# Expert gate and up products as three single-pass products of high and low parts, with one set of weight buffers and a new order of the jobs

## The reference, cut to what matters

```python
def hier_moe(h, w_rg, w_re, w_gate, w_up, w_down):      # h: tokens x 1024
    g_idx = jnp.argmax(h @ w_rg, axis=-1)               # best of 4 groups
    ...
    top_v, top_i = lax.top_k(e_in_group, TOP_K)         # best 2 of its 8 experts
    w = jax.nn.softmax(top_v, axis=-1) * g_w
    flat_e = (g_idx[:, None] * EXPERTS_PER_GROUP + top_i).reshape(-1)
    order = jnp.argsort(flat_e)
    ...
    a = lax.ragged_dot(xs, w_gate, sizes)               # 1024 -> 512 of each row's own expert, 32 experts
    u = lax.ragged_dot(xs, w_up, sizes)                 # 1024 -> 512
    y = lax.ragged_dot(jax.nn.silu(a) * u, w_down, sizes)   # 512 -> 1024
    y = y * w.reshape(-1)[order][:, None].astype(y.dtype)
    return jax.ops.segment_sum(y, tok, num_segments=n)
```

## Time and profile before

| What | us |
|---|---|
| Median of three runs | 6089.7 |
| The profiled execution, its own time | 6090.85 |
| Its span in the trace | 6089.3 |
| TensorE busy | 5199.9 |
| VectorE busy | 2233.9 |
| ScalarE busy | 1677.5 |
| GpSimd busy | 821.7 |

### The profile page before, as it was taken

One profiled execution on the slowest core, in us unless ns is written; L12 is line 12 of the kernel. 1 busy time (PEld: TensorE's weight loads), 2 busy tenths in 40 slices (PEclk: granted clock), 3 DMA queues, 4 the chain that ended last, 5 costly groups with the idle time before them and its releaser, 6 DMA issues. The chain is left out here.

```text
span 6089.3 us, 76302 instructions
## 1 busy us (share of the span) xinstructions
PE 5199.9 (85%) x27165; PEld 3869.3 (64%) x27165; DVE 2233.9 (37%) x4438; ACT 1677.5 (28%) x2876; POOL 821.7 (13%) x1023
## 2 busy tenths in 40 slices
PE   9588899779789885999991888979879886999995
PEld 1388889669668763444441888978778665444442
DVE  0455155566443432111115552547553333111113
ACT  0244254446322320000001342536542221000000
POOL 0244200440000001000001440006200001000001
PEclk9799999899899997999995999989889998999998
DMA  8432451324332464899976432233343343999997
GB/s 320 175 92 88 145 172 47 95 72 111 135 147 98 167 202 165 326 335 334 334 281 229 144 95 78 68 81 78 90 134 114 143 148 110 343 334 335 334 334 265
DMA packets 610733, 1111.26 MB, mean 182 GB/s; under 512 B 108400, under 2 KB 291984, under 8 KB 610032
## 3 DMA queue, kind: packets, MB, share of 16 engines
q1 hardware_dynamic: 565104, 956.50, 47.0%
q0 software_dynamic: 29504, 94.50, 4.0%
q10 hardware_dynamic: 15936, 57.78, 2.3%
HBM read 908.23 MB, written 200.45 MB: 182 GB/s over the span
## 5 line engine op out<-in xcount | busy, mean ns | idle before, releaser
L642 PE MATMUL project_proj_acc<-project_w_split,project_hT 128*128 128x256 f32 x5472 | 720.0, 291 | 41.0 <-DVE project_w_split L527 41.0
L642 PEld LDWEIGHTS project_proj_acc<-project_w_split,project_hT 128*128 128x128 f32 x5472 | 689.5, 198 | 42.1 <-DVE project_w_split L527 41.8
L1452 PE MATMUL merge_acc<-merge_hT,merge_w_split 128*128 128x512 f32 (+1 forms) x2880 | 633.4, 376 | 20.0 <-issue 16.8
L1452 PEld LDWEIGHTS merge_acc<-merge_hT,merge_w_split 128*128 128x128 f32 x2880 | 507.9, 190 | 128.9 <-issue 22.0
L2059 PE MATMUL experts_gate_acc<-experts_w_gate,experts_rowsT 128*128 128x512 f32 x1184 | 526.0, 597 | 6.9 <-DMA experts_w_up<-in_w_exp_up_dram 6.9
L2046 PE MATMUL experts_result_acc<-experts_w_down,experts_hiddenT 128*128 128x512 f32 x1184 | 520.5, 592 | 2.4 <-DVE experts_hiddenT L2018 2.4
L2064 PE MATMUL experts_up_acc<-experts_w_up,experts_rowsT 128*128 128x512 f32 x1184 | 520.2, 592 | 0.0
L2064 PEld LDWEIGHTS experts_up_acc<-experts_w_up,experts_rowsT 128*128 128x128 f32 x1184 | 225.0, 190 | 283.2 <-issue 283.2
L2010 DVE TENSOR_TENSOR experts_hidden<-experts_silu_gate,experts_up_acc 128x512 f32<-128x512 f32 x74 | 50.9, 688 | 964.5 <-PE experts_up_acc L2064 515.4
L2059 PEld LDWEIGHTS experts_gate_acc<-experts_w_gate,experts_rowsT 128*128 128x128 f32 x1184 | 221.2, 192 | 259.1 <-issue 257.4
L2046 PEld LDWEIGHTS experts_result_acc<-experts_w_down,experts_hiddenT 128*128 128x128 f32 x1184 | 219.3, 190 | 251.6 <-issue 248.7
(11 more groups left out here) (207 smaller groups left out, 7401.2 us busy)
## 6 DMA issues: line engine op xcount, KB each, us to landing
experts_w_gate<-in_w_exp_gate_dram SPq DMA_DIRECT2D x74, 2048.0 KB, 13.8
experts_w_up<-in_w_exp_up_dram SPq DMA_DIRECT2D x74, 2048.0 KB, 18.8
experts_w_down<-in_w_exp_down_dram SPq DMA_DIRECT2D x74, 2048.0 KB, 9.8
merge_w_raw<-in_w_merge_dram SPq DMA_DIRECT2D x120, 768.0 KB, 6.6
modulation_w_ada<-in_w_ada_dram SPq DMA_DIRECT2D x24, 2048.0 KB, 7.8
qk<-project_staged SPq DMA_DIRECT2D x168, 256.0 KB, 2.3
ye<-experts_result ACTq DMA_DIRECT2D x74, 512.0 KB, 8.2
ye<-attend_a_zeros POOLq DMA_DIRECT2D x52, 512.0 KB, 27.3
```

The lines of the kernel that those rows point to most:

```text
L642: m = pe.matmul(acc[s % 4][:, 0:HALF], hT[:, a, k, t * P:(t + 1) * P], w_split[hf][:, c, k, :], start=(i == 0 and k == 0), stop=(i == 2 an ...
L1452: m = pe.matmul(acc[:, bank, 0:w], w_split[b][:, a, k0 + k, :], act_T[:, x, kk, 0:w], start=(i == 0 and k == 0), stop=(i == 2 and k == n - 1))
```

## The change

The two sets of weight buffers go. There is now one buffer per weight, `raw`, in two halves of 1 MB, each with its own load and semaphore, and beside it one fp32r buffer `w` for gate and one for up that holds high and low parts. ScalarE casts each half to the high part, VectorE subtracts to get the low part, and TensorE makes 24 single-pass matmuls for gate and 24 for up; down stays in fp32 and reads `raw` itself. The transposed rows get high and low parts too. ScalarE alone now copies the result.

The raw buffers outlive `deal_rows`, which loads the three weights of expert 0 for job 0. For this the first 32 jobs are fixed as the first 128 rows of experts 0 to 31, and only the further tiles of larger experts are listed behind them; `deal_rows` gets some more VectorE steps for it. GpSimd issues the gathers of jobs 0 and 1 ahead of its loop.

```diff
 SP in deal_rows
+            for n in range(3):
+                for half in range(2):
+                    sp.dma_start(raw[n][:, half, :], expert_half(io, l, slice(0, 1), n, half)
+                                 ).then_inc(raw_in[n][half].sem, 16)
 VectorE in deal_rows
-            step(dve.tensor_scalar(base[:, :], base[:, :], float(P), None, ALU.mult))
-            step(dve.tensor_tensor(place[:, :, :], acc[:, 0:nq, :],
+            step(dve.tensor_tensor(base[:, :], base[:, :], small[:, C_JOB:C_JOB + NE], ALU.subtract))
+            step(dve.tensor_scalar(base[:, :], base[:, :], float(NE - 1), float(P), ALU.add, ALU.mult))
+            step(dve.tensor_scalar(place[:, :, :], acc[:, 0:nq, :], float(P), None, ALU.is_ge))
+            step(dve.tensor_tensor(place[:, :, :], place[:, :, :],
+                                   base[:, :].unsqueeze(1).to_broadcast([P, nq, NE]), ALU.mult))
+            step(dve.tensor_tensor(place[:, :, :], acc[:, 0:nq, :], place[:, :, :], ALU.add))
+            step(dve.tensor_scalar(base[:, :], small[:, C_JOB:C_JOB + NE], float(P), None, ALU.mult))
+            step(dve.tensor_tensor(place[:, :, :], place[:, :, :],
 run_experts
-    lo, hi = nq, MAX_JOBS // 2
-    w_gate = [sb(f"w_gate{b}", [P, KD, EH]) for b in range(2)]
-    w_up = [sb(f"w_up{b}", [P, KD, EH]) for b in range(2)]
-    w_down = [sb(f"w_down{b}", [P, HK, D]) for b in range(2)]
+    PASSES = ((0, 0), (1, 0), (0, 1))
+    lo, hi = NE // 2, MAX_JOBS // 2
+    w = [sb(f"w_{n}", [P, 2, 2, 2048], F32R) for n in ("gate", "up")]
 SP
-                    if later(g, 2):
-                        sp.wait_ge(um.sem, um.done(g - 2))
-                    for w, name in ((w_gate, "w_exp_gate"), (w_up, "w_exp_up")):
-                        sp.dma_start(w[b][:, :, :], io[name][l, ds(e, 1), :, :].rearrange(
-                            "o (k p) n -> p (o k) n", p=P)).then_inc(gu_in[b].sem, 16)
-                    if later(g, 2):
-                        sp.wait_ge(dm.sem, dm.done(g - 2))
+                    for n in range(3):
+                        for half in range(2):
+                            if n == DOWN:
+                                sp.wait_ge(dm.sem, dm.done(g - 1))
+                            else:
+                                sp.wait_ge(w_lo[n].sem, w_lo[n].done(g * 2 + half - 2))
+                            sp.dma_start(raw[n][:, half, :], expert_half(io, l, ds(e, 1), n, half)
+                                         ).then_inc(raw_in[n][half].sem, 16)
 ScalarE
+            def split(n, g):
+                if later(g, 1):
+                    act.wait_ge(products[n].sem, products[n].done(g - 1))
+                for half in range(2):
+                    act.wait_ge(raw_in[n][half].sem, raw_in[n][half].done(g))
+                    act.copy(w[n][:, 0, half, :], raw[n][:, half, :]).then_inc(w_hi[n].sem, 1)
...
                     act.activation(act_g[:, :], acc_g[:, :], ACT.Silu).then_inc(sg.sem, 1)
                     if not (last and b):
-                        copy_rows(g + 1)
+                        split(GATE, g + 1)
+                        rows_hi(g + 1)
+                        split(UP, g + 1)
 VectorE
+                    if not (last and b):
+                        split(GATE, g + 1)
                     dve.wait_ge(sg.sem, sg.done(g))
                     dve.wait_ge(um.sem, um.done(g))
...
                     dve.tensor_tensor(hidden[:, :], act_g[:, :], acc_u[:, :], ALU.mult).then_inc(hm.sem, 1)
                     if not (last and b):
-                        copy_rows(g + 1)
-                    if not isinstance(g, int) or g > 0:
-                        result(g - 1, 1 - b, i if b else i - 1)
+                        rows_lo(g + 1)
+                        split(UP, g + 1)
 TensorE
+            def into_hidden(n, acc, g):
+                for half in range(2):
+                    pe.wait_ge(w_lo[n].sem, w_lo[n].done(g * 2 + half))
+                    for i, (a, c) in enumerate(PASSES):
+                        for k in range(KD // 2):
+                            m = pe.matmul(acc[:, :], xT[:, a, half * (KD // 2) + k, :],
+                                          w[n][:, c, half, k * EH:(k + 1) * EH], start=(half == 0 and i == 0 and k == 0),
+                                          stop=(half == 1 and i == 2 and k == KD // 2 - 1))
+                m.then_inc(products[n].sem, 1)
...
-                    for k in range(KD):
-                        m = pe.matmul(acc_g[:, :], xT[:, k, :], w_gate[b][:, k, :], start=(k == 0), stop=(k == KD - 1))
-                    m.then_inc(gm.sem, 1)
+                    into_hidden(GATE, acc_g, g)
```

More of the change, by code:

```diff
@@ L1492, in stage_experts @@
             output_and_route(nc, io, scr, l, nq, st, inner, ident, logits)
[L1493 to L1496, removed]
+        with ExitStack() as weights:
+            raw = [st.sb(f"raw_{n}", [P, 2, 2048], F32, weights) for n in ("gate", "up", "down")]
+            raw_in = [[st.dma(f"raw_{n}{half}_loaded") for half in range(2)] for n in ("gate", "up", "down")]
+            with ExitStack() as inner:
+                deal_rows(nc, io, scr, l, nq, st, inner, logits, row_of, weight, jobs, more_pairs, raw, raw_in)
+            with ExitStack() as inner:
+                run_experts(nc, io, scr, l, nq, st, inner, ident, jobs, more_pairs, raw, raw_in)
         with ExitStack() as inner:
@@ L1816, in _ @@
             step(dve.tensor_copy(base[:, :], acc[:, nq, :]))
-            step(dve.tensor_tensor(more[:, :, :], base[:, :].unsqueeze(2).to_broadcast([P, NE, NT]),
-                                   small[:, C_TILE:C_TILE + NT].unsqueeze(1).to_broadcast([P, NE, NT]), ALU.is_gt))
+            step(dve.tensor_tensor(more[:, :, :], base[:, :].unsqueeze(2).to_broadcast([P, NE, NT - 1]),
+                                   small[:, C_TILE + 1:C_TILE + NT].unsqueeze(1).to_broadcast([P, NE, NT - 1]),
+                                   ALU.is_gt))
             step(dve.tensor_reduce(tiles[:, :], more[:, :, :], AX.X, ALU.add))
@@ L1870, in _, with expert_half, run_experts @@
             pool.wait_ge(scat.sem, scat.done(2 * nq - 1))
-def run_experts(nc, io, scr, l, nq, st, inner, ident, jobs, more_pairs):
+def expert_half(io, l, e, n, half):
+    w = io[("w_exp_gate", "w_exp_up", "w_exp_down")[n]]
+    rows = w.shape[2] // 2
+    return w[l, e, half * rows:(half + 1) * rows, :].rearrange("o (k p) n -> p (o k) n", p=P)
+def run_experts(nc, io, scr, l, nq, st, inner, ident, jobs, more_pairs, raw, raw_in):
     def sb(name, shape, dt=F32):
@@ L2035, in transpose_rows, with down @@
                 m.then_inc(xt.sem, 1)
-            def down(g, b, i):
+            def into_hidden(n, acc, g):
+                for half in range(2):
+                    pe.wait_ge(w_lo[n].sem, w_lo[n].done(g * 2 + half))
[5 more added lines that the diff above has]
+                m.then_inc(products[n].sem, 1)
+            def down(g):
                 pe.wait_ge(hc.sem, hc.done(g))
-                pe.wait_ge(d_in[b].sem, d_in[b].done(i))
-                if later(g, 1):
-                    pe.wait_ge(ya.sem, ya.done(g - 1))
                 if later(g, 1):
                     pe.wait_ge(yd.sem, yd.done(g - 1))
-                for h in range(D // 512):
-                    for k in range(HK):
-                        m = pe.matmul(acc_y[:, h * 512:(h + 1) * 512], hT[b][:, k, :],
-                                      w_down[b][:, k, h * 512:(h + 1) * 512], start=(k == 0), stop=(k == HK - 1))
+                for half in range(2):
+                    pe.wait_ge(raw_in[DOWN][half].sem, raw_in[DOWN][half].done(g))
+                    for c0 in range(D // 512):
+                        for k in range(HK // 2):
+                            m = pe.matmul(acc_y[:, c0 * 512:(c0 + 1) * 512], hT[:, half * (HK // 2) + k, :],
+                                          raw[DOWN][:, half, k * D + c0 * 512:k * D + (c0 + 1) * 512],
+                                          start=(half == 0 and k == 0), stop=(half == 1 and k == HK // 2 - 1))
                 m.then_inc(dm.sem, 1)
@@ L2076, in _ @@
             transpose_rows(0, 0, 0)
-            pairs(pe, n, body)
-            down(n * 2 - 1, 1, n - 1)
+            pairs(pe, n_pairs, body)
+            down(n_pairs * 2 - 1)
 def combine(nc, io, scr, l, nq, st, inner, row_of, weight, out):
```

144 lines of the change are left out of this document (75 added, 69 removed).

## The result

The changed kernel takes 7408.9 us, median of four runs (7400.3 to 7417.4); the kernel before, run beside it, takes 6089.0 (6085.6 to 6094.5, four runs). The ratio is 1.217, 95% interval 1.215 to 1.219. The forecast was 7450, range 7280 to 7620. The profiled execution took 7408.05 us, of which 7406.5 are span.

What follows compares the result with a forecast made beforehand. TensorE bounds the kernel before; the change puts load, split and TensorE's work in series. 2887.5 + 100 - 1630.8 + 4 = +1361, with 6090.85 giving 7452, less 1.2 for the median: 7450 us, range 7280 to 7620.

Steps and rivals of the forecast that it cites:

- SP's wait as the cause: SP's in-order queue: next gate and up loads stand behind the wait for down(g-1), putting load, split and products in series.
- The load, 0.15 + 13.4: After down(g-1) ends: SP wakes in 0.15 us, four halves (4 MB) land in 13.4, bounds 13.0 to 15.3.
- the rival in which all halves land together: Weight loads: engines shared among six halves, gate's second landing at 18.6 us; period 46.5, about 7815 us; chance 0.06.
- The split and what follows, 6.3: ScalarE and VectorE before gate(g+1): second half's cast and subtraction, hidden, transposed rows' subtraction, semaphores; 6.3 us.
- TensorE's 19.2: TensorE's work per period: gate 5.6, up 5.6, transposed rows 0.9, down 6.9, 0.2 until its end is seen.
- the clock's 2.2: Gate products after TensorE's rest: restarting at 1.2 GHz costs between 1.6 and 2.9 us each time; 2.2 taken.
- The rival of the full clock: TensorE after its rest: the clock stays full, period 39.05 us, 7297 us in all; chance 0.10.
- The period: Expert loops, end of one job's down to the next: 41.25 us in place of 21.91, 70 times, 2887.5 us.
- Head and tail: Each layer's start until down(0) ends, 36.1 us, and last down products with their load, 14; twice 50.1 is 100.
- Dealing, +4, preload 0: Before the expert loops: extra dealing steps cost 4 us over both layers; loading job 0 early counts 0, bounds -6 and +3.
- TensorE sets the pace: Rival for the expert loops: gate load out of SP's way, 19.4 us per job, 5905 us; chance 0.04.
- What would have shown it: Profile signs: TensorE busy about 21 of 41 us, gap near 19 ended by rows' low part, DMA near 178 GB/s.

Runs made afterwards that it cites:

- The filler: Changed kernel with 80 unread fp32 128x128 identity matmuls on TensorE behind each down(g-1): 7281.7 us (single).
- Both cures: Changed kernel with SP issuing the next gate and up loads before down: 5992.5 us; or with two down buffers, SP's order kept: 5971.3 us.

## Why the prediction was right, point by point

**SP's wait as the cause: shown.** Its total rose from 1127.6 to 2469.8 us; turning the order gives 5992, a second down buffer 5971, and taking the buffers from the kernel before costs 1617 us by itself, with the old products and the old dealing.

**The load, 0.15 + 13.4:** the cast of the second half begins 13.3 us after T (6516.07 to 6529.33), so the choice near the low end of 13.0 to 15.3 was right. The order of landings of the earlier trace rows held too, 10.5 and 13.3, and the rival in which all halves land together (7815 us) fell.

**The split and what follows, 6.3:** 6.1 (6529.33 to 6535.41). Together 19.3 from T to gate in place of 19.85.

**TensorE's 19.2 and the clock's 2.2:** 21.6 in the timeline, 0.2 above their sum. Gate takes 8.10 from start to start where up takes 5.6; over the kernel the difference of the two groups is 2.2 per job. The rival of the full clock (7297 us) fell by the 0.50 in the window. The filler brings about its state and takes about 150 us out of the loops, against the 154 (70 x 2.2) by which that rival stood below the forecast.

**The period:** from the end of down(0) to that of down(N-2) it is 40.72 us in layer 1 (34 of them) and 40.64 in layer 2 (36), against 41.25. That makes the forecast 40 us too high. In the period shown T to gate is 0.5 below the forecast and TensorE's part 0.2 above it; the mean period is 0.3 shorter still, and gate's mean price is 2.2, not the 2.5 of this period. The other terms nearly cancel: head and tail are 2 us longer than forecast, all else 6 shorter, as told below.

**Head and tail:** 36.5 in both layers (36.1 forecast). The tail, from layer 1's last load to its last product:

```profile
3825.98 0.89 SPq L1958 DMA_DIRECT2D experts_raw_down<-in_w_exp_down_dram  x2
3831.32 10.12 PE L2102 MATMUL experts_result_acc<-experts_raw_down,experts_hiddenT 128*128 128x512 f32 x16 [4.94 <-DMA experts_raw_down<-in_w_exp_down_dram]
```

It is 15.5 here and 13.9 in layer 2 (14 forecast). The first half lands 5.3 us after its issue, and 16 matmuls take 10.12 rather than 7.03: the granted clock is 0.50 until 3837, 0.91 in the two us behind it and then 1.00.

**Dealing, +4, preload 0:** the stretch from dealing's first load to the first gate product grew by 0.2 us in layer 1 and shrank by 0.3 in layer 2. The longer chain of steps was forecast at +4 and the preload at 0; together they came to nothing, so the preload hid about what the steps cost. That term was wrong by 4 us of 1361. From first gate to last down the layers take 1436.6 and 1513.4 us, 1319.2 more than before; the span grew by 1317.2, so all that lies outside is 2 us shorter. The old dealing under two down buffers shows that preload and new dealing are worth about 11 us in two layers, once a split is there to hide.

**TensorE sets the pace (5905 us, 0.04):** wrong for the change, right for the kernel that it could have been. The condition was that the gate load be out of SP's way, at least 19.4 us earlier. Both cures send it one job earlier and still stop at 20.2 us. By the prediction's own terms the chain of 19.85 us would have fitted into the 20.2 at hand; it took 21.3, because the second gate half was there 15.2 us after the wait and not 13.3. The second half of up was still landing then (its cast waits until 5410.18); that this is what delays gate was not tested. With hidden and rows moved ahead as well the 19.4 per job and 5913 us are there.

**What would have shown it:** TensorE busy 21 of 41 us was 22.9 (0.56 x 40.9), since the slow gate counts as busy; DMA mean 177 to 179 GB/s for 178. The gap was 18.1 and not 19, and was booked to hidden ahead of the transposes and not to the rows, though the chain is the one forecast.

## What to carry to other kernels

When a buffer is taken away, look not only at who waits for it but at what stands behind that wait in the same in-order queue: a wait that was harmless at 16 us cost 1317 us when the next job's first load stood behind it, and asking for that load first takes 1416 us off without any memory. Then put the operations that need no load, here hidden and the rows, ahead of those that wait for one. A DMA share near 1 over many jobs is not proof of a cap: windows shorter than a job show whether the queue runs dry.

## What the runs showed that was not expected

- The same loads read as 360 GB/s at a share of 0.99 and as 379 at 1.02, since the job became shorter; inside one job 123 and 409 stand side by side.
- SP's own time counts: behind a wait, its second pair of loads went out 1.8 to 2.1 us after the first. That fits why 2 MB less in front of gate saved 3.1 us and not 5.2.
- Eighty small fp32 matmuls per job, read by nobody, paid for themselves: about 150 us less in the loops for 24 more at the two ends.
